# Moving POOL's steps and the small products of an SSD scan inside the query and key passes of a hybrid decoder layer

## The reference, cut to what matters

```python
CB = jnp.einsum('bclgn,bcsgn->bcgls', Cc, Bc)
y_diag = jnp.einsum('bcgls,bcgrls,bcsgrp->bclgrp', CB, decay, Xdt)
states = jnp.einsum('bclgn,bclgr,bclgrp->bcgrpn', Bc, decay_to_end, Xdt)
h_0, h_1, ... = scan over chunks: h = chunk_decay * h + states
y_off = jnp.einsum('bclgn,bcgrpn,bclgr->bclgrp', Cc, h_in, jnp.exp(cum))
y = y_diag + y_off + X * d_skip
y_ssm = rmsnorm(y * silu(z), ssm_norm_w)
q = rmsnorm(q, q_norm_w);  k = rmsnorm(k, k_norm_w)      # per head
```

## Time and profile before

| | before |
|---|---|
| median of 3 runs | 721.67 us (721.09 to 723.37) |
| the profiled execution | 722.29 us |
| its span, first to last instruction | 720.6 us |
| TensorE busy | 679.8 us, 94% |
| VectorE, ScalarE, POOL busy | 389.4, 291.4, 132.3 us |

### The profile page before, as it was taken

One profiled execution on the slowest core, in us unless ns is written; L12 is line 12 of the kernel. 1 busy time (PEld: TensorE's weight loads), 2 busy tenths in 40 slices (PEclk: granted clock), 3 DMA queues, 4 the chain that ended last, 5 costly groups with the idle time before them and its releaser, 6 DMA issues.

```text
span 720.6 us, 10643 instructions
## 1 busy us (share of the span) xinstructions
PE 679.8 (94%) x3850; PEld 470.5 (65%) x3850; DVE 389.4 (54%) x845; ACT 291.4 (40%) x651; POOL 132.3 (18%) x167
## 2 busy tenths in 40 slices
PE   8999999999999999999999999989999978878975
PEld 7878888777777888767767788877434323323542
DVE  6866678878879665777887643471222211212211
ACT  5934534465555546665676423221212111202200
POOL 2300010114222120022223110020132321122331
PEclk9999999999999999999999999979999989989998
DMA  8333255426254343191020079689999999999993
GB/s 297 95 115 117 77 175 162 131 74 176 82 153 146 88 146 104 45 362 46 19 100 2 10 291 424 241 335 376 412 417 416 403 409 399 424 418 414 412 403 120
DMA packets 61159, 162.77 MB, mean 226 GB/s; under 512 B 14184, under 2 KB 25604, under 8 KB 49840
## 3 DMA queue, kind: packets, MB, share of 16 engines
q1 hardware_dynamic: 49120, 144.64, 53.6%
q0 software_dynamic: 6880, 9.02, 4.3%
q10 hardware_dynamic: 5104, 8.39, 3.2%
HBM read 157.67 MB, written 20.28 MB: 247 GB/s over the span
## 4 chain that ended last, share of the span: by engine, by line
PE 27%; DMA 9%; SPq 9%; DVE 2%; issue 2%; ACT 1%; POOL 0%; POOLq 0%; DVEq 0%; ACTq 0%
PE bank L1813 6%; DMA s_gu<-in_w_expert_gate_dram 4%; SPq L427 4%; DMA s_gu<-in_w_expert_up_dram 4%; PE bank L1842 3%; PE bank L1402 3%; PE bank L1404 3%; PE bank L1403 3%; SPq L475 2%; SPq L461 2%; PE bank L1784 2%; PE bank L1678 1%; PE bank L1635 1%; PE bank L1618 1%; PE bank L1760 1%
## 5 line engine op out<-in xcount | busy, mean ns | idle before, releaser
L1813 PE MATMUL bank<-s_gu,s_xgT 128*64 128x512 f32 x352 | 84.6, 636 | 15.8 <-DMA s_gu<-in_w_expert_up_dram 15.8
L282 DVE TENSOR_TENSOR s_wl<-s_raw,s_wh 128x512 fp32r<-128x512 f32 x116 | 91.6, 836 | 11.8 <-ACT s_wh L1019 11.5
L1019 ACT ACTIVATE s_wh<-s_raw 128x512 fp32r<-128x512 f32 x120 | 72.6, 627 | 42.1 <-PE bank L1404 18.6
L1402 PE MATMUL bank<-s_wh,s_hTh 128*128 128x512 f32 x192 | 78.7, 410 | 0.0
L1404 PE MATMUL bank<-s_wh,s_hTl 128*128 128x512 f32 x192 | 75.2, 391 | 0.0
L1403 PE MATMUL bank<-s_wl,s_hTh 128*128 128x512 f32 x192 | 74.8, 390 | 0.0
L1813 PEld LDWEIGHTS bank<-s_gu,s_xgT 128*64 128x64 f32 x352 | 28.4, 146 | 70.9 <-issue 70.9
L1318 ACT ACTIVATE s_sg<-bank,s_slot_scale 128x256 f32<-128x256 f32 x16 | 7.6, 474 | 151.7 <-PE bank L1813 104.5
L1842 PE MATMUL bank<-s_dn,s_hidT 128*64 128x512 f32 x256 | 58.5, 598 | 1.6 <-DVE s_hidT L2385 1.6
L2385 DVE COPY s_hidT<-bank 128x256 f32<-128x256 f32 x16 | 6.8, 424 | 92.9 <-PE bank L1822 92.9
L2418 DVE SCALAR_TENSOR_TENSOR s_yrow<-bank,s_slot_scale,s_xg 128x512 f32<-128x512 f32 x30 | 21.2, 746 | 46.4 <-PE bank L1842 46.4
(11 more groups left out here) (307 smaller groups left out, 1372.2 us busy)
## 6 DMA issues: line engine op xcount, KB each, us to landing
s_dn<-in_w_expert_down_dram SPq DMA_DIRECT2D x28, 1024.0 KB
s_gu<-in_w_expert_gate_dram SPq DMA_DIRECT2D x26, 1024.0 KB
s_gu<-in_w_expert_up_dram SPq DMA_DIRECT2D x24, 1024.0 KB, 30.2
s_raw<-in_w_in_dram SPq DMA_DIRECT2D x88, 256.0 KB, 4.4
s_raw<-in_w_out_dram SPq DMA_DIRECT2D x32, 256.0 KB, 3.4
s_gu<-in_w_expert_up_dram SPq DMA_DIRECT2D x12, 512.0 KB
s_decay_rows<-decay_rows SPq DMA_DIRECT2D x4, 1024.0 KB, 4.6
s_gu<-in_w_expert_gate_dram SPq DMA_DIRECT2D x8, 512.0 KB
```

What stands on the lines that cost most here:

```text
L282: eng.tensor_tensor(low, full, high.bitcast(F32), ALU.subtract).then_inc(sem(f"{what}_low_{low_engine(what, i)}"), 1)
L1019: act.activation(wh[:, i % HL, :], raw[:, i % RAW, :], ACT.Copy).then_inc(sem("w_high"), 1)
L1402: pe.matmul(dst, ah, bh, start=start, stop=False)
L1813: last = pe.matmul(ps[j][r, :].rearrange("p (w f) -> p w f", w=2), m["xgT"][:, j, k, r], gu[:, half, :, k, :], start=(k == 0), stop=(k == ...
```

## The change

- TensorE: cb(0) stands behind slot 3 of pass 1, not slot 1. diag(c,0) and diag(c,1) stand behind slots 2 and 4 of pass 4c+2, not 1 and 3. diag(c,2) and diag(c,3) stand behind slots 1 and 3 of pass 4c+3, and y_off(c,1) behind its slot 4; they stood together with the transposes after pass 4c+2.
- POOL: gate(c) waits for the same sums of y as before (chunk 0 counts no y_whole now, so the values are lower by 2), but also for the state's update of its chunk (state_kept), the last one for the sums of pass 15. scaled_x(c) waits for the chunk's four M products and stands behind skip_term.
- SP: decay_out(c) and the first bias rows are released by what y_whole or y_diag say then (chunk 0 counts no y_whole any more). decay_out(c) is released by chunk c-1's y.
- ScalarE: the square of pass 0 stands ahead of the table load; the two exponentials of dte and etot behind the first two decays.
- VectorE: chunk 0's copy of y onto itself is gone; the product of dte stands behind the first two M products.

```diff
             def load_decay_out(c):
-                sp.wait_ge(sem("y_whole"), 2 * c)
+                if c == 1:
+                    sp.wait_ge(sem("y_diag"), 2)
+                else:
+                    sp.wait_ge(sem("y_whole"), 2 * (c - 1))
...
             def load_first_bias():
-                sp.wait_ge(sem("y_whole"), 2 * TC)
+                sp.wait_ge(sem("y_whole"), 2 * (TC - 1))
...
             def scaled_x(c):
                 if c < TC - 1:
+                    pool.wait_ge(sem("m_done"), 4 * c + 4)
                     if c:
                         pool.wait_ge(sem("state_done"), 2 * c)
...
             def gate(c):
-                pool.wait_ge(sem("y_whole"), 2 * c + 2)
+                if c:
+                    pool.wait_ge(sem("y_whole"), 2 * c)
+                else:
+                    pool.wait_ge(sem("y_diag"), 2)
+                if c < TC - 1:
+                    pool.wait_ge(sem("state_kept"), 2 * c + 2)
+                else:
+                    pool.wait_ge(sem("qk_sum"), 16)
...
                 causal_decays(c + 1)
                 gate(c)
+                skip_term(c + 1)
                 scaled_x(c + 1)
-                skip_term(c + 1)
...
+            qk_square(0)
             act.preload_act_table_set("natural_log_exp_and_others")
-            act.wait_ge(sem("steps_known"), 4)
-            act.activation(dte[:], dte[:], ACT.Exp).then_inc(sem("dt_acts"), 1)
-            act.activation(etot[:], tot[:, :, 0:H], ACT.Exp).then_inc(sem("dt_acts"), 1)
             for i in range(16):
                 n = N_QK + i
-                qk_square(i)
+                if i:
+                    qk_square(i)
...
                     if i:
                         decay_out_exp(i // 4)
+                    else:
+                        act.wait_ge(sem("steps_known"), 4)
+                        act.activation(dte[:], dte[:], ACT.Exp).then_inc(sem("dt_acts"), 1)
+                        act.activation(etot[:], tot[:, :, 0:H], ACT.Exp).then_inc(sem("dt_acts"), 1)
...
-                    if i == 1 and k == 1:
+                    if i == 1 and k == 3:
                         cb(0)
-                    if i >= 2 and i % 4 == 2 and k in (1, 3):
-                        diag(i // 4, k // 2)
+                    if i >= 2 and i % 4 == 2 and k in (2, 4):
+                        diag(i // 4, k // 2 - 1)
+                    if i >= 2 and i % 4 == 3 and k in (1, 3):
+                        diag(i // 4, 2 + k // 2)
+                    if i > 4 and i % 4 == 3 and k == 4:
+                        y_off(i // 4, 1)
...
-                if step == 1:
-                    if c:
-                        y_off(c, 1)
-                    diag(c, 2)
-                    diag(c, 3)
...
-                else:
-                    dve.tensor_copy(y[:, cols], y[:, cols]).then_inc(sem("y_whole"), 1)
...
-                if i == 0:
-                    dve.wait_ge(sem("dt_acts"), 5)
-                    dve.tensor_tensor(dte[:], dte[:], sp[:, :, 0:H], ALU.mult).then_inc(sem("scales_known"), 1)
-                    dve.wait_ge(sem("scales_known"), 1)
                 c = i // 4
                 if i % 4 == 0:
                     m_product(c, 0)
                     m_product(c, 1)
+                    if c == 0:
+                        dve.wait_ge(sem("dt_acts"), 5)
+                        dve.tensor_tensor(dte[:], dte[:], sp[:, :, 0:H], ALU.mult).then_inc(sem("scales_known"), 1)
+                        dve.wait_ge(sem("scales_known"), 1)
```

## The result

| | before | after |
|---|---|---|
| median of 8 runs each, same chip | 722.56 us (721.09 to 724.34) | 726.16 us (723.72 to 727.76) |
| ratio after/before | | 1.0046, 95% interval 1.003 to 1.0062 |
| the profiled execution | 722.29 us | 723.72 us |

The change costs 3.3 us by the ratio, 0.46%, and the whole interval lies on the slower side. The forecast was 721.2 us, range 719.0 to 724.2.

A forecast was written before the change was run, and what follows sets the result against it. TensorE, busy 679.8 of 720.6 us, was taken as the bound. Removing 4.3 us of stalls and adding 3.9 us (1.56 + 0.6 + 1.6 + 0.1) gave 0.45 us gained: median 721.2 us, range 719.0 to 724.2.

The forecast's parts named there:

- The bound and the pass-through: Whole kernel: TensorE, busy 679.8 of 720.6 us, bounds it; scan gains or losses reach the end one for one.
- The six old stalls: Six places in the scan where TensorE waits for late operands; 4.3 us removed, low bound 3.1 us.
- The lows: VectorE's seven low parts of weight slots per chunk; left alone by POOL they take 4.3 us.
- The ring: Scan, through four engines: gating, loads, decays, y, lows, state's update; 26.0 us plus load landing, against TensorE's own 31.1 us.
- x: Scan, from gating's end until conv and decay_out have landed: 5.9 us, bounds 4.0 and 10.1; over 5.1 TensorE waits.
- ring waits: diag(c,2) in chunks 2 and 3 waits 0.8 us, twice: 1.6 us added.
- the last transposes: After the scan's last pass, the lows leave these about 0.1 us late.
- the price of spreading: Small products set apart in the fourth passes: 1.56 us added for diag 2 and 3, 0.6 us for y_off.
- (b): Rival: decay_out lands as slowly as in its old place, x 8.7 us; 5.15 us lost, 726.8 us; chance 0.12.
- (a): Rival: transfers hidden, x at or under 5.1 us, no new wait; 2.05 us gained, 719.6 us; chance 0.30.
- (c): Rival: POOL's moved instructions block VectorE's two-input work, ring grows 1.9 us; 3.35 us lost, 725.0 us; chance 0.06.
- the 0.6 us for a low issued together with gating: Scan: the low may take the port first, making gating and transfers 0.6 us later, twice; median 722.4 us, not added.

The follow-up runs named there:

- experiment 7: The changed kernel with gating no longer waiting for the state's update: 723.4 us, ratio 1.002.
- experiment 1: The changed kernel with SP issuing decay_out ahead of the conv load: 719.6 us, ratio 0.9957; measured again, 719.37 us, 0.9965.
- experiment 3: The changed kernel with ScalarE making decay_out's exponential behind the chunk's last two decays, SP's order unchanged: 719.85 us, ratio 0.9961.
- experiment 5: The changed kernel with decay_out ahead of conv, and diag(c,2), diag(c,3), y_off(c,1) joined again behind pass 4c+2: 718.64 us, ratio 0.9952.
- experiment 2: The changed kernel with the four weight slots behind decay_out issued ahead of both conv load and decay_out: 725.85 us, ratio 1.0039.
- experiment 4: The changed kernel with diag(c,2), diag(c,3) and y_off(c,1) joined again behind pass 4c+2, all else kept: 725.79 us, ratio 1.0053.
- experiment 6: The kernel before with only TensorE's part of the change (small products spread or placed later): 729.46 us, ratio 1.0101.
- experiment 8: The changed kernel with four weight slots issued between the conv load and decay_out: 734.88 us, ratio 1.0177.

## Why the prediction was wrong

**Right.** The bound and the pass-through: the end of the scan's shift reached the router whole (2.9 us). The six old stalls went, all of them; that holding gating back is what keeps those behind chunks 0 and 1 away is shown by experiment 7, where they return. The lows came down from 8.21 us for seven to 3.70 for six plus one. The ring was the right mechanism, with the right members, in the right chunks (2 and 3, not 1). Its segments in chunk 1 to 2:

| segment | predicted | measured |
|---|---|---|
| diag(1,2) to the lows | 6.1 | 192.94 - 186.90 = 6.0 |
| low 1 to the seventh high | 3.4 | 3.5 |
| high and low | 1.25 | 1.3 |
| reduction to the state kept | 4.8 | 4.8 |
| gating to its end | 2.9 | 3.0 |
| **x** | **5.9** | **212.83 - 205.46 = 7.4** |
| exponential to the end of the decays | 5.7 | 5.7 |
| last M product and y's add, to diag(2,2) | 1.85 | 220.41 - 218.50 = 1.9 |
| sum | 31.9 | 33.5 |
| TensorE's own way | 31.1 | 30.9 |

**The step that failed** is the size of x: "Taking the backlog (6.7 less 3.9, the middle and the least of conv) from decay_out's middle 7.3 leaves 4.5". The load lands 5.3 us after its issue with no conv load ahead of it (experiment 1), 5.7 right behind the conv load, and the exponential needs the later of two halves: issued at 205.95 + 0.64 = 206.6, read at 212.83, 6.2 us. So x is 1.1 + 6.2, not 1.4 + 4.5. The backlog of one load was taken from another of other shape: 2.8 us, the spread between the conv load's middle and least, where the move from the old place to the new one was worth 7.3 - 5.7 = 1.6. The bound of 10.1 was sound. The earlier trace rows had decay_out's least at 6.3; with it x is 7.7, and the waits 2 x 2.6 = 5.2 us, which is what was measured. I held the emptier queue to be a better neighbour than the load's own least time. "Loses more than the 0.3% once x is over 7.2" held: x was 7.4.

**The sum, term by term,** at the end of the scan (start of the first product behind pass 15's transposes: 267.16 us after, 264.26 before, +2.9). Experiment 3's trace runs 0.2 us ahead of both from the start (first product behind the first transposes at 119.36, against 119.61 and 119.58), and that is taken off:
- ring waits 1.6 predicted, 5.2 measured (pass 16 starts at 260.87 in after and at 255.41 in experiment 3, which has no ring; 2.6 and 2.65 by the chunks above);
- the last transposes 0.1 predicted; they cost 0.71 in after and 0.35 before, 0.36;
- six stalls less the price of spreading: 4.3 - 2.16 = 2.1 predicted; pass 16 starts at 258.33 before and at 255.41 in experiment 3: 2.7. If the 4.3 is right the price is 1.6, not 2.16. The pieces agree: 0.69 for each diag, 0.82 for y_off, 0.35 for the transposes, 2.55 against 2.45 joined, and a tenth more in the distance behind each of the first pass products, three more times; some 0.4 us per chunk, 0.3 in chunk 0. In experiment 5 the joined cluster took 2.67, not 2.45; why y_off ran longer there stays open.

So -0.45 became -2.7 + 5.2 + 0.4 = +2.9. The rest of the miss of 5.0 us (726.2 for 721.2): the kernel before had a median of 722.56 in the longer comparison where 721.67 was shown, 0.9 us; and 0.7 us between the 3.6 of the medians and the trace's 2.9. The cause of that is not shown, but there is a likely one that I had overlooked, the clock. After's trace has two waits of 1.91 us and the granted clock stayed at 1.00 behind both; behind such waits it fell to half in the traces of experiments 2 (granted clock 0.55 from 254 to 257 us), 4, 6 (0.56 from 208 to 211) and 8, at 1.5 to 1.6 us each in 2, 4 and 8, and in the scan of no other trace (experiment 6's waits there were 1.24 and 0.66 us). Some of after's other executions may have paid that; no trace shows it.

**Rivals.** (b), decay_out as the new bound, had the right mechanism, with x 1.3 too long. That its time of 726.8 lies so near is in part luck: it was +5.15 us on 721.67, and +3.3 on 722.56 was measured. (a) is what experiments 1 and 3 make: 719.4 to 719.9, for 719.6 worked out. (c) did not occur: X scaling stretched the last step of y_add(c,0) from 0.69 to 1.18 us in chunk 1 and 1.17 in chunk 2, where VectorE had time for it. Nor did the 0.6 us for a low issued together with gating come on top: gating took 2.85 us beside such a low, as in the row of before, and 2.39 where it came first (experiment 1, the last gating, at 260.27; the low at 261.75 then took 1.46). The rule of the Trainium skill, "SBUF — State Buffer", section "Who interferes with whom", is borne out once more by experiment 7: lows with two SBUF inputs beside one gating, 6.45 us for seven, and 4.4 where gating is held back.

**What is open.** Why decay_out lands 1.2 us later than the conv load (5.7 against 4.5, medians of after) was not taken apart: a half of it and a conv chunk differ in their layout, in the spreading over partitions and in their place in the queue at once. Nor was it tried on another queue.

## What to carry to other kernels

An order held back to save one engine holds back everything that is queued behind its reader: follow each queue past the moved step once all the way round, and ask of every load in it whether it needs that wait at all. If such a ring is within a few us of the bounding engine's own way, size its longest unknown by that operation's own least time in the trace, not by what another one seems to gain from an empty queue. And a part of a change that shows no difference when undone alone (joining, here) can be worth something once the wait that covers it is gone: undo it again with the main cause repaired, and look at the granted clock behind each wait before comparing two traces.

## What the runs showed of the hardware

decay_out is loaded in two halves, each spread over 64 partitions. The median from issue to landing was
- 5.3 us with four weight loads issued just ahead and no conv load (experiment 1);
- 5.7 us right behind the conv load, with four weight loads behind (after), and 5.5 without those (experiment 2);
- 6.2 us behind the conv load and then four weight loads, issued within 2.0 us (experiment 8);
- 7.3 and 7.4 us behind four weight loads issued over 4.3 us and then the conv load (before, experiment 7).

So neither kind of load ahead of it makes the long time alone. No run has this load in an empty queue, so its own least time stays open.

Behind a wait of TensorE of about 2 us the granted clock sometimes fell to half for some 3 us: not in after (two waits of 1.91 us, 1.00), once in experiment 2, in experiment 4 (1.83 us, then 0.51) and in experiment 8 (2.62 and 1.92 us, then 0.50 in chunk 2; the same waits in chunk 3 and 1.00).
